# Expert blocks that fetch their tokens by column copies on GpSimd instead of by a one-hot product on TensorE

## The reference, cut to what matters

```
logits = ht @ w_router + b_router              # 256 tokens, 32 experts
top_val, top_idx = top_k(logits, 4); gates = softmax(top_val)
for each expert e, for its tokens x:           # 1024 to 2048, then 1024 to 1024
    hg = x @ w_gu[e] + b_gu[e]
    act = min(glu, 7) * sigmoid(1.702 * glu) * (clip(lin, -7, 7) + 1)
    out[token] += gate * (act @ w_down[e] + b_down[e])
```

## Time and profile before

| what | value |
|---|---|
| time, median of 3 runs | 2367.64 us (2366.95 to 2368.96) |
| the profiled execution | 2370.77 us; its span 2368.8 us |
| TensorE busy | 2289.1 us (97%) |
| VectorE, ScalarE, GpSimd busy | 34%, 16%, 0% |
| mean DMA rate over the span | 254 GB/s |
| loads of `w_gu` and `w_down` | 384 of 1 MiB each |
| costliest group | line 951, 128x512 products of `wring` and `big`, x3456, 770.3 us |

### The profile page before, as it was taken

One profiled execution on the slowest core, in us unless ns is written; L12 is line 12 of the kernel. 1 busy time (PEld: TensorE's weight loads), 2 busy tenths in 40 slices (PEclk: granted clock), 3 DMA queues, 4 the chain that ended last, 5 costly groups with the idle time before them and its releaser, 6 DMA issues.

```text
span 2368.8 us, 29374 instructions
## 1 busy us (share of the span) xinstructions
PE 2289.1 (97%) x11382; PEld 1306.8 (55%) x11383; DVE 798.8 (34%) x1686; ACT 388.3 (16%) x849; POOL 5.3 (0%) x11
## 2 busy tenths in 40 slices
PE   6999999999999989999999899999999999999998
PEld 3564458888544678998888433333333333333333
DVE  1134545555651335873133321221121122121112
ACT  3222221111001312220233200000000000000001
POOL 0000000000000000000000000000000000000000
PEclk9999999999999999999999899999999999999999
DMA  9711342222684506448941499999896979999895
GB/s 380 242 66 54 115 130 81 84 89 85 198 283 136 186 18 196 162 162 299 294 146 64 179 421 422 422 422 422 365 391 257 422 301 422 422 422 422 344 423 230
DMA packets 196204, 602.75 MB, mean 254 GB/s; under 512 B 11042, under 2 KB 128034, under 8 KB 146850
## 3 DMA queue, kind: packets, MB, share of 16 engines
q1 hardware_dynamic: 193728, 599.04, 66.2%
q10 hardware_dynamic: 2402, 2.67, 0.4%
HBM read 600.62 MB, written 1.05 MB: 254 GB/s over the span
## 4 chain that ended last, share of the span: by engine, by line
PE 86%; DMA 8%; ACT 2%; DVE 2%; SPq 1%; issue 1%; POOL 0%; DVEq 0%; POOLq 0%; ACTq 0%
PE bank L359 52%; PE bank L951 33%; DMA wring<-in_w_gu 7%; SPq L2141 1%; ACT big L1104 1%; DMA wring<-in_ev_w_in 1%; PE bank L983 1%; ACT hT L1104 1%; PE bank L976 0%; DVE wring L1518 0%; ACT tmp L1104 0%; DVE big L1518 0%; DVE tmp L1518 0%; PE bank L654 0%; POOL xT L2131 0%
## 5 line engine op out<-in xcount | busy, mean ns | idle before, releaser
L951 PE MATMUL bank<-wring,big 128*64 128x512 f32 x3456 | 770.3, 596 | 21.3 <-DMA wring<-in_w_gu 11.4
L951 PEld LDWEIGHTS bank<-wring,big 128*64 128x64 f32 x3456 | 235.9, 137 | 504.3 <-issue 451.1
L359 PE MATMUL bank<-hT,wring 128*128 128x256 f32 (+2 forms) x1888 | 456.1, 395 | 6.3 <-ACT hT L1104 4.6
L359 PEld LDWEIGHTS bank<-hT,wring 128*128 128x128 f32 x1888 | 322.1, 192 | 123.0 <-issue 85.3
L359 PE MATMUL bank<-big,wring 128*128 128x256 f32 (+1 forms) x1096 | 346.0, 477 | 6.4 <-DVE big L1521 3.5
L359 PEld LDWEIGHTS bank<-big,wring 128*128 128x128 f32 x1096 | 209.6, 192 | 139.4 <-issue 115.7
L359 PE MATMUL bank<-wring 128*128 128x256 f32 (+1 forms) x1408 | 246.2, 328 | 0.9 <-DVE wring L1518 0.8
L1104 ACT ACTIVATE big<-bank 128x256 f32<-128x256 f32 (+3 forms) x238 | 108.0, 454 | 830.5 <-PE bank L976 432.7
L359 PEld LDWEIGHTS bank<-wring 128*128 128x128 f32 x1408 | 216.5, 191 | 20.2 <-DVE wring L1518 1.3
L1521 DVE TENSOR_SCALAR big<-bank 128x512 f32<-128x512 f32 (+1 forms) x73 | 50.0, 684 | 467.1 <-PE bank L951 466.7
L951 PE MATMUL bank<-big 64*128 64x256 f32 (+1 forms) x872 | 141.1, 462 | 1.6 <-DVE big L1521 1.1
(11 more groups left out here) (156 smaller groups left out, 1188.4 us busy)
## 6 DMA issues: line engine op xcount, KB each, us to landing
wring<-in_w_gu SPq DMA_DIRECT2D x256, 1024.0 KB, 15.5
wring<-in_w_down SPq DMA_DIRECT2D x128, 1024.0 KB, 14.5
wring<-in_ffn_w_up SPq DMA_DIRECT2D x44, 1024.0 KB, 5.1
wring<-in_mod_w SPq DMA_DIRECT2D x24, 1024.0 KB, 15.2
wring<-in_mod_w SPq DMA_DIRECT2D x48, 512.0 KB, 4.6
wring<-in_ffn_w_down SPq DMA_DIRECT2D x16, 1024.0 KB, 5.2
wring<-in_w_ada SPq DMA_DIRECT2D x16, 1024.0 KB, 5.1
wring<-in_w_in SPq DMA_DIRECT2D x14, 1024.0 KB, 11.9
```

The source lines that it names most:

```text
L359: ins = pe.matmul(o, l, r, start=start, stop=stop, skip_group_check=True)
L951: ins = pe.matmul(o, l, r, start=start, stop=stop, skip_group_check=True)
```

## The change

The two-step fetch (product and four transposes) stays for blocks 0 and 1. For blocks from 2 on:

- TensorE multiplies `SEL` with a column of token numbers (`IDS`) instead of with `H2`. This gives one row of 64 token numbers in `bank[7]` (`token_ids`; an empty slot gives 0). It also raises `moe_used`. The numbers for block b + 2 are made in turn b, one block earlier than the rows were.
- VectorE copies that row to SBUF as integers (`take_ids`), behind `activate` and ahead of `one_hot`; `take_x` leaves the loop.
- GpSimd has a loop of its own. In each turn it waits for the row and for `XN` to be free, does one tiny add (`PACE`), and then, for four groups of 16, loads 16 numbers into registers and makes 16 copies. One copy moves one token's column out of `hT` (the hidden state with features on the partitions): 128 partitions by 8 elements, strided on both sides, the source address taken from a register.
- ScalarE copies `XN` to `XG` (`take_columns`) behind the sigmoid, once `gate_up` of the present block is through; this takes the place of `take_rows_x`.
- In block 0, `down` is cut into two halves with `token_ids` for block 2 between them.

```
+            def token_ids(sels, inc):
+                pe.wait_ge(G("m_sel"), sels)
+                for tt in range(2):
+                    xmm(bank[7][0:1, 0:CAP], IDS[:, tt:tt + 1], SEL[:, tt, :], tt == 0, tt == 1,
+                        G("m_rows") if tt else inc)
...
                 pe.wait_ge(G("m_sgt"), b)
-                gather(b + 2, G("moe_used"))
+                token_ids(b + 3, G("moe_used"))
                 pe.wait_ge(G("m_yk"), b)
                 scatter()
                 pe.wait_ge(G("m_act"), b + 1)
                 turn_act()
-                pe.wait_ge(G("m_rows_out"), b + 2)
-                flip(bank[7], XS, 4, G("m_x"))
                 pe.wait_ge(G("m_ac"), b + 1)
                 down(e)
...
+            def take_columns(n):
+                act.wait_ge(G("m_xn"), n - 2)
+                act.wait_ge(G("m_lin"), n - 1)
+                A(XG, XN, ACT.Copy).then_inc(G("m_xg"), 1)
...
-                take_rows_x(b + 2)
+                take_columns(b + 2)
...
+            def take_ids(n, held):
+                dve.wait_ge(G("m_rows"), n + 1)
+                if held is not None:
+                    dve.wait_ge(G("m_xn"), held)
+                v.tensor_copy(ITOK[0:1, :], bank[7][0:1, 0:CAP]).then_inc(G("m_tok"), 1)
...
-                take_x(b + 1)
                 take_y(b)
                 gselect(ep, b - 1, b)
-                dve.wait_ge(G("m_rows"), b + 1)
-                select(en, b + 1)
+                dve.wait_ge(G("m_rows"), b + 2)
+                select(es, b + 2)
                 activate(b + 1)
+                take_ids(b + 2, b)
                 one_hot(en)
...
+            with pool.Fori(1, nblk) as b:
+                pool.wait_ge(G("m_tok"), b)
+                pool.wait_ge(G("m_xg"), b + 1)
+                pool.tensor_tensor(PACE, IDS[0:1, 0:1], IDS[0:1, 1:2], ALU.add)
+                for g in range(CAP // 16):
+                    _, toks = nc.values_load_multi_w_load_instructions(
+                        ITOK[0:1, 16 * g:16 * g + 16], engines=[pool.engine], min_val=0, max_val=S - 1, ...)
+                    for i, t in enumerate(toks):
+                        s = 16 * g + i
+                        ins = pool.tensor_copy(target[:, :, :, s:s + 1], source[:, :, :, bass.ds(t, 1)])
+                ins.then_inc(G("m_xn"), 1)
```

More of the change, by code:

```diff
@@ L280, in program @@
         XG = big[:, 5, :]
+        XN = big[:, 20, :]
+        IDS = big[:, 14, 2 * NE + 4:2 * NE + 6]
+        PACE = big[0:1, 14, 2 * NE + 6:2 * NE + 7]
+        ITOK = rows.rearrange("p a b -> p (a b)")[:, 512 - CAP:512].bitcast(I32)
         GL = big[:, 6, :]
@@ L1004, in gate_up, with down @@
                         xmm(halves(bank[4 + q // 2], q % 2), kchunk(XG, t), ws[:, T2 * q:T2 * q + T2], t == 0, t == 7, inc)
-            def down(e):
-                for s in range(4):
+            def down(e, ss=range(4)):
+                for s in ss:
                     ws = wslot(GUC + s, e).rearrange("p (j n) -> p j n", j=2)
@@ L1052, in _ @@
             pe.wait_ge(G("m_ac"), 1)
-            down(0)
+            down(0, range(2))
+            pe.wait_ge(G("m_xg"), 2)
+            token_ids(3, None)
+            down(0, range(2, 4))
             with pe.Fori(1, nblk) as b:
@@ L2021, in _ @@
             TS(sm[:, 126:127], sm[:, 32:33], 1.0, None, MUL).then_inc(G("diag"), 1)
+            for tt in range(2):
+                TS(IDS[:, tt:tt + 1], minus_p, -1.0, float(P * tt), MUL, ADD)
             TS(itab[:, 1, 0:NE], cum, -1.0, None, ADD)
@@ L2094, in _ @@
             one_hot(e1)
+            e2 = dve.value_load(itab[0:1, 0, 2:3], min_val=0, max_val=NE - 1)
+            dve.wait_ge(G("m_rows"), 2)
+            select(e2, 2)
+            take_x(2)
+            take_ids(2, None)
             with dve.Fori(1, nblk) as b:
@@ L2097, in _ @@
                 en = dve.value_load(itab[0:1, 0, bass.ds(b + 1, 1)], min_val=0, max_val=NE - 1)
-                take_x(b + 1)
+                es = dve.value_load(itab[0:1, 0, bass.ds(b + 2, 1)], min_val=0, max_val=NE - 1)
                 take_y(b)
                 gselect(ep, b - 1, b)
-                dve.wait_ge(G("m_rows"), b + 1)
-                select(en, b + 1)
+                dve.wait_ge(G("m_rows"), b + 2)
+                select(es, b + 2)
                 activate(b + 1)
+                take_ids(b + 2, b)
                 one_hot(en)
@@ L2107, in _ @@
             el = dve.value_load(itab[0:1, 0, bass.ds(nblk - 1, 1)], min_val=0, max_val=NE - 1)
-            take_x(nblk + 1)
             gselect(el, nblk - 1, nblk)
@@ L2128, in _ @@
         def _(pool):
+            source = hT.rearrange("p (i c) t -> p i c t", i=2)
+            target = XN.rearrange("p (c i s) -> p i c s", c=4, i=2)
+            pool.wait_ge(G("tables"), 2)
+            nblk = pool.value_load(itab[0:1, 2, MAXB:MAXB + 1], min_val=NE, max_val=MAXB - 1)
+            with pool.Fori(1, nblk) as b:
[4 more added lines that the diff above has]
+                    _, toks = nc.values_load_multi_w_load_instructions(
+                        ITOK[0:1, 16 * g:16 * g + 16], engines=[pool.engine], min_val=0, max_val=S - 1,
+                        skip_runtime_bounds_check_because="each is 0 or the number of one token, below S")
+                    for i, t in enumerate(toks):
+                        s = 16 * g + i
+                        ins = pool.tensor_copy(target[:, :, :, s:s + 1], source[:, :, :, bass.ds(t, 1)])
+                ins.then_inc(G("m_xn"), 1)
             for c in range(DC - 1):
```

## The result

The changed kernel takes 2347.07 us (2346.73 to 2348.74, 4 runs) against 2368.3 of the kernel before beside it (2366.95 to 2369.65): a ratio of 0.9912 [0.9895, 0.9929], 21.2 us less. The forecast was 2349.6, in a range of 2345 to 2367. The profiled execution of the changed kernel took 2346.73 us, its span 2344.7, its mean granted clock 0.991.

The account below looks back on a forecast made before the run. TensorE at 27.52 us a block bounds the expert stage, the weight stream its unbroken stretches. Savings of 1.2, 9.6, 1.2 and 6.0 us sum to 18.0, giving 2349.6 us from the median 2367.64; range 2345 to 2367.

Parts of the forecast that it names:

- What was removed: TensorE, each block: gather's 1.8 us leaves the way to turn_act; removing flip's four transposes (0.60 us) gives nothing.
- What was late next: Before turn_act: VectorE's product, ready at 1390.76, limits the saving to 1.27 us; 1.2 taken, period 26.3 us.
- the ends of 0 and 0.6: TensorE's added token_ids: nothing if wholly overlapped, 0.6 us as four passes of 0.15; 0.3 taken.
- GpSimd's price: GpSimd per block: copies 12.8 us, loads 1.2, rest 0.5, together 14.5 us; ends 3.6 and 65.7.
- 11 us to spare: GpSimd's turn of 14.5 us stays hidden, since up to about 26 us costs nothing.
- The break-even turn: Rival, GpSimd becomes the bound: costs from 26.1 us a turn, eats all the gain at 27.3; chance 0.17.
- The prediction's estimate by the page: GpSimd's loads at 200 ns a register: 12.8 us, turn 26.1, period 26.8, gain about 10 us, 2358 us.
- VectorE beside GpSimd: Rival: GpSimd's copies keep VectorE's gselect from SBUF, TensorE stands still 2.9 us a block, 2410 us; chance 0.05.
- The sum: Expert stage: 1.2 us at block 12, 9.6 to block 21's restart, 1.2 at block 30, 6.0 for 31 to 35; 18.0 us.
- the two ends of stretches bound by weights: Blocks 0 to 12 and block 21's restart to block 30: weights bind, only 1.2 us saved at each end.
- The stream: Weight stream, 29.8 us an expert, turns savings between its pauses into waiting; rival that it hides nothing: 2324 us, chance 0.02.

Follow-up runs that it names:

- e1: Changed kernel with the four one-hot products put back ahead of the token numbers, result unused: 2373.56 us, 1.0023.
- e2: Changed kernel with four transposes of a 128x512 tile put back between turn_act and down, result unused: 2349.24 us, 0.992.
- e8: Changed kernel with gate_up's last eight products reordered and the sigmoid's product made early, one VectorE instruction less before turn_act: 2348.55 us, 0.9914.
- e3: Changed kernel with each column copied twice by GpSimd, the extra copy to a buffer nobody reads: 2348.29 us, 0.9922.
- e4: Changed kernel with each column copied three times by GpSimd, the extra two to buffers nobody reads: 2385.49 us, 1.008.
- e7: Changed kernel with one register load per token, 64 a block, in place of four loads of 16: 2396.76 us, 1.0123.
- e11: The changed kernel itself timed and profiled again, nothing edited: 2348.39 us, 0.9917.
- e5: Kernel before, with SP loading only half of each weight piece from the second expert on: 2350.31 us, 0.9925.
- e6: Changed kernel, with SP loading only half of each weight piece from the second expert on: 2306.96 us, 0.9743.

## Why the prediction was right

**What was removed.** `gather` was the saving (e1) and the four transposes none (e2), each as forecast.

**What was late next.** The wait for VectorE's product was named, at 1.27 us of saving at most; 1.26 was measured (27.52 to 26.26). The forecast also saw how close behind it TensorE's own end stood: 0.16 us (1390.6 against 1390.76), where e8 gave 0.15. That `token_ids`, whose shape no row had, came out at 0.31 for the 0.3 taken between the ends of 0 and 0.6 is luck, but by the forecast's own sum either end would have moved the period by some 0.1 us at most.

**GpSimd's price.** The copies were taken at 0.20 us and are 0.130 apart; the loads at 0.306 for 16 and take 1.056. Both were wrong, by -4.5 and +3.0 us a turn, and another 1.0 goes because GpSimd stands idle for only 0.70 to 0.97 us of each load; that the sum, 12.0 for 14.5, came as near as it did is in part luck. It changed nothing, as there were 11 us to spare. That this slack was real, e3 (18.3 us, free), e4 and e7 (27.5 and 28, slower) show from either side; no run lies between 18.3 and 27.5, so where exactly it ends was not measured. The break-even turn had been put at 27.3 us. By that e4, 0.2 past the edge, would lose 35 x 0.2 = 7 us against 979.4; its stage is 14.4 longer. At 28.31 us, 35 periods make 991, which is 11.5 of them: a little more than 0.7 lies between turn and period. The other 2.9 lie at the two ends of the stage (5.9 us from block 0's `turn_act` to the first turn, 25.3 from the last turn's start to block 35's `turn_act`, together 2.9 more than a period). The stream has no part in it: e4's chain of waits names GpSimd throughout the stage and no load of weights.

The Trainium skill, Runtime: NRT & Kernel Launch, section Instruction fetch mechanics, gives about 200 ns for a register, in bulk too; its section Terms says that these loads come from HBM, and those here come from SBUF. The trace shows 66 ns each in a load of 16; of a single one, 286 ns, the page's figure is nearer. The prediction's estimate by the page, half the gain lost, also took the copies at 0.20 us. With the measured 0.130, 64 registers at the page's figure and 64 copies make some 21 us, an estimate, and the gain would have been kept.

**VectorE beside GpSimd.** `gselect` was not held up, neither in the changed kernel nor in e4, where copies run beside it without a gap (0.60 and 0.48 us at 1801.04 and 1801.80). Where VectorE's instructions read two large operands in SBUF (e4, 1785.28 and 1786.01), GpSimd's copy is the one that waits, 0.73 and 0.66 us in place of 0.20, and VectorE keeps its 0.69. The Trainium skill, SBUF — State Buffer, section Who interferes with whom, has the first to come hold the port for its whole instruction; these rows agree for the order in which VectorE comes first (1785.28 before 1785.30, 1786.01 before 1786.10) and show no case in which a copy holds VectorE up.

**The sum.** It was 2.7 us short. The period's 1.26 for 1.2 makes 0.8 of that over the 13 blocks. The rest lies at the two ends of stretches bound by weights, -1.9 and -2.4 us, where 1.2 each was forecast. The forecast took the stream to start at the same time and run at the same rate. SP's rows of the two kernels for the expert that follows block 21's restart, and the windows from 3 to 23 us behind that restart, show otherwise; first before, then after:

```profile
1958.58 6.32 SPq L2141 DMA_DIRECT2D wring<-in_w_down  x4
```

```profile
1940.94:1960.94 20.00, 19.75 (x103) 7.95 (x104) 3.60 (x6) 2.21 (x4) 0.00 (x0) 1.00 0.98 395
```

```profile
1922.55 14.23 SPq L2187 DMA_DIRECT2D wring<-in_w_gu  x8
...
1941.93 6.33 SPq L2187 DMA_DIRECT2D wring<-in_w_down  x4
```

```profile
1925.55:1945.55 20.00, 19.24 (x101) 7.59 (x102) 3.02 (x6) 2.13 (x4) 4.49 (x33) 1.00 1.00 411
```

The slots of `down` come free 19.38 us behind the first issue, where it was 20.64 (the earlier trace rows has the start), because TensorE passes the same place 1.2 us sooner. The stream that had stood idle meanwhile moves (411 - 395) x 20 us = 0.32 MB more, 0.76 us at 422 GB/s. By this estimate the last weights of the stretch land that much earlier, and 1.26 + 0.76 = 2.0 us is what its end should gain. Measured were 2.4 there. The chain of waits shows where they lie; its last wait for weights in the stretch, before and after:

```profile
2173.94 26.84 DMA wring<-in_w_gu
```

```profile
2156.78 27.43 DMA wring<-in_w_gu
```

It ends 273.19 us behind block 20's `turn_act` before and 272.07 after, so the weights are there 1.1 us earlier, of which the 0.76 explains the greater part; from there to block 30's `turn_act` it is 5.62 and 4.30, the 1.3 of the shorter way. At the first stretch the 1.9 are 0.6 and 1.3 in the same way (the waits end at 1701.82 and 1697.76); why the weights come 0.6 earlier there was not followed. In a second profile of the changed kernel (e11) the two ends gain 2.2 and 1.7, so a few tenths are spread.

**The stream.** Half the gain goes to it, as forecast: 43 us of saving without it, 21 with it (e5, e6).

## What to carry to other kernels

Where two resources run nearly level, count a saving by the stretches between two stops of the slower one: here 13 of 35 blocks kept their 1.26 us and the other 22 only the ends of their stretches. Shortening a consumer also frees the producer's buffers sooner, so look at where the producer stands and waits. Before work is moved to an idle engine, work out the turn at which it begins to decide; with a wide gap to it, prices off by a third and by a factor of three did no harm here, and one load for many registers in place of many loads can be the whole gap.

## What the runs showed of the hardware

GpSimd starts a copy of 128 x 8 float32, with its source address in a register, every 0.130 us, though one lasts 0.197. A load of 16 registers from SBUF takes it 1.056 us, one of a single register 0.286, and when more copies are queued the load passes beside them (e3: 140 loads of 1.057 us, 34.9 us of idle time). TensorE's granted clock went from 1.00 to 0.50 behind a standstill of 2.80 us that followed a stretch in which it was busy throughout (e4, block 15), and its first 40 products then took 11.80 us for 8.80; behind another standstill of 2.80 us in the same run (block 32) it stayed at 1.00 and they took 8.80. Behind the 0.69 us ahead of `down` in the changed kernel they took 8.80 as well. A copy on GpSimd beside a two-operand instruction of VectorE took 0.73 and 0.66 us in place of 0.20, and VectorE's instruction kept its 0.69 (e4).
